# Seams of a two-layer diffusion block on one core: gate rows in pieces behind other products, projections and the last dense unit tile by tile, routing ahead of splits

## The chip, the cores and the metric

The kernel runs on one core of a Trainium2 chip. Its engines are TensorE (PE in the profile, with PEld for its weight loads), VectorE (DVE), ScalarE (ACT), GpSimd (POOL) and SyncE (SP, which here only issues transfers). The metric is the device time of one execution in microseconds (us).

## The reference

Two layers over 256 latent tokens x and 256 context tokens xc of width 1024, all in fp32:

```python
# even layer, for latent and context tokens (each with its own modulation)
h = modulate(rms_norm(x, norm_mix), sh1, sc1) @ w_in          # 1024 -> 2048
u, q, k, v = split(h)                                         # 4 x 128 Fourier groups | 8 heads of 64
q, k = rms_norm(q, q_gain), rms_norm(k, k_gain)
x = x + g1 * (concat(fourier_mix(u), attention(q, k, v)) @ w_out)
x = x + g2 * ((silu(h2 @ w1) * (h2 @ w3)) @ w2)               # h2 = modulate(rms_norm(x, ..)), width 2816
# odd layer, latent tokens only at its end
h = modulate(rms_norm(x, norm_mix), sh1, sc1) @ w_in          # attention (12/3 heads, rotary) | S5 recurrence
x = x + g1 * (concat(o_attn, o_ssm) @ w_out)
t = modulate(rms_norm(x, norm_ffn), sh2, sc2)
logits = t @ router_w + router_b; top 2 of 8, softmax over the two
x = x + g2 * sum_e gate_e * ((silu(t @ w1[e]) * (t @ w3[e])) @ w2[e])   # width 3584
```

`modulate(h, shift, scale)` is `h * (1 + scale) + shift`, and g1, g2 are gate vectors of width 1024 from the same conditioning.

## The kernel before

Tokens lie in four tiles of 128 (two latent, two context), features on the free side in X; SyncE streams all weights through a ring of three slots of 2 MB (six halves). Each engine's program is written out by hand, and semaphores join them; nothing is reordered by a scheduler. Dense and expert weights are split into two fp32r parts, WR (ScalarE, a copy) and rest (VectorE, a difference), and each product is three passes over them, in units of one ring half. Such a unit is written `split`, and three or four are prepared ahead of the dense part and of the experts.

The places that the change touches, in order of time:

- **q/k gains of the even layer.** GpSimd makes sixteen products of the S5 tables (L1870 to L1875, each stored by a transfer, L1876), then multiplies q and k by their gains (L1883, eight tiles, `head_ready`), then loads the biases of the attention (L1894). TensorE's transposes of q and k (L571) wait for the gains.
- **Gate rows.** A gate vector lies over partitions, in `mod`. To multiply with it, TensorE makes from it a row that is equal in all partitions (L656: four products of 128 columns into bank 7 for half a row) and ScalarE copies it out (L1134). `gate_rows(q)` makes all rows of gate q together: 4 for q = 0 and 1, 2 for q = 2 and 3. Each waits until ScalarE has emptied bank 7. They stand before the even and the odd output projection, before the dense part, and before the router's products.
- **Output projection** (`w_out`, L674). One bank of 128 tokens by 512 columns at a time, in banks 3 to 6 in turn: first the left half for all tiles, then the right half. VectorE multiplies each bank with its gate row (`gated_sum`, L1381) into one of two buffers, and GpSimd adds it to X (`residual`, L1760).
- **Norms.** `squares` (ScalarE) waits for all residuals, squares each tile and adds it up (L1034), then one Sqrt for all (L1024); `normed` (VectorE) makes mean, reciprocal (L1312, L1314) and scales the tiles (L1352); TensorE transposes them (`norm_turn`, L534, banks 0 to 3), ScalarE and VectorE modulate in turn (L1048, L1363), and ahead of the dense part they also split the result into hTr (L1054, L1369).
- **Dense part** (`dense_swiglu`). Units "up" (L695) and "down" (L713); the last unit goes over its two 128-row slices and, inside, over the four tiles, so that all four banks end together.
- **Routing.** VectorE clears acc, ye and part of pick (L1614 to L1616), makes two splits (L1594), then takes the logits (L892) and goes through top 2, ranks (L900) and the pick tables (L1714); TensorE gathers with them (L911), and the first expert begins (L938).

## Time and profile before

| | |
|---|---|
| Median of 3 runs | 2031.52 us (2027.45 to 2033.12) |
| The profiled execution's own time | 2027.75 us |
| Its span in the trace | 2026.0 us |
| Busy share PE / DVE / ACT / POOL | 93% / 61% / 48% / 15% |
| Mean granted TensorE clock | 0.964 of full speed |

Times in the trace are microseconds from the start of its span. The granted clock is 1.00 at 2.4 GHz and 0.50 at 1.2 GHz. A busy TensorE isn't TensorE at its peak: matmuls overlap, and their ends are modelled.

### The profile page before, as it was taken

The page shows a single profiled execution, that of the slowest core. Times are in us where ns is not written, and L with a number is a line of the kernel's source. Part 1 is how long each engine was busy: PE and PEld are TensorE (multiplying, and loading weights), DVE is VectorE, ACT ScalarE, POOL GpSimd, SP SyncE. Part 2 cuts the span into 40 slices and gives each one's busy share as a digit, 9 for nine tenths or more (in the row PEclk, how much of TensorE's full clock was granted, in tenths as well). Part 3 has the DMA queues.
Part 4 walks back from the last instruction along what each step waited for, and adds up shares of the span by engine and source line. Part 5 has one row for each costly group of instructions (what it writes and reads, how often), then busy time and mean ns, then how long its engine had stood idle before and what let it go on. Part 6 is the DMA issues. An engine that isn't in the chain of part 4 may idle for free.

```text
span 2026.0 us, 25076 instructions
## 1 busy us (share of the span) xinstructions
PE 1887.9 (93%) x8946; PEld 1422.5 (70%) x8946; DVE 1232.6 (61%) x1303; ACT 974.5 (48%) x1051; POOL 306.0 (15%) x584
## 2 busy tenths in 40 slices
PE   5999989699999996879599999999999999999997
PEld 3445554687878784645578888788887878878785
DVE  2121641333332322383688888988989889888996
ACT  2011330421222212243367777777776777776773
POOL 6887702002020202401000000000000000000000
PEclk8998999799999998989699999999999999999999
DMA  9254981122221225141189899998999989999994
GB/s 373 99 221 121 353 353 42 42 104 83 87 101 66 100 84 181 23 135 42 42 335 373 340 357 353 344 373 325 370 354 343 374 323 369 355 346 352 345 366 161
DMA packets 72087, 481.69 MB, mean 238 GB/s; under 512 B 8336, under 2 KB 11536, under 8 KB 17168
## 3 DMA queue, kind: packets, MB, share of 16 engines
q1 hardware_dynamic: 67888, 468.73, 60.7%
q0 software_dynamic: 2448, 7.61, 1.4%
q10 hardware_dynamic: 1680, 4.43, 0.6%
q8 instruction: 42, 0.69, 0.1%
q14 instruction: 29, 0.24, 0.0%
HBM read 473.41 MB, written 7.32 MB: 237 GB/s over the span
## 4 chain that ended last, share of the span: by engine, by line
PE 83%; POOL 7%; DVE 4%; issue 2%; ACT 2%; DMA 1%; ACTq 0%; DVEq 0%; POOLq 0%
PE bank L938 30%; PE bank L952 15%; PE bank L695 12%; PE bank L713 6%; PE bank L674 4%; PE bank L751 3%; PE bank L911 2%; PE bank L975 2%; PE bank L507 2%; PE bank L921 1%; PE bank L639 1%; PE bank L622 1%; POOL X L1760 1%; PE bank L656 1%; PE bank L534 1%
## 5 line engine op out<-in xcount | busy, mean ns | idle before, releaser
L1594 DVE TENSOR_TENSOR rest<-ring,WR 128x2048 fp32r<-128x2048 f32 x336 | 758.7, 2289 | 101.4 <-ACT WR L1214 100.9
L1214 ACT ACTIVATE WR<-ring 128x2048 fp32r<-128x2048 f32 x336 | 632.9, 1917 | 51.0 <-DMA ring<-in_experts 50.2
L938 PE MATMUL bank<-WR,xer 128*128 128x512 f32 x1792 | 588.0, 400 | 4.7 <-DVE xer L1682 4.7
L938 PEld LDWEIGHTS bank<-WR,xer 128*128 128x128 f32 x1792 | 337.7, 188 | 76.6 <-issue 8.8
L938 PE MATMUL bank<-rest,xer 128*128 128x512 f32 x896 | 350.5, 391 | 0.0
L952 PE MATMUL bank<-WR,heTr 128*128 128x512 f32 x896 | 281.9, 392 | 0.0
L695 PE MATMUL bank<-hTr,WR 128*128 128x512 f32 x704 | 222.0, 397 | 12.5 <-DVE tmpf L1381 12.5
L938 PEld LDWEIGHTS bank<-rest,xer 128*128 128x128 f32 x896 | 169.3, 189 | 36.2 <-issue 3.8
L952 PEld LDWEIGHTS bank<-WR,heTr 128*128 128x128 f32 x896 | 168.2, 188 | 34.3
L952 PE MATMUL bank<-rest,heTr 128*128 128x512 f32 x448 | 174.5, 389 | 0.0
L695 PEld LDWEIGHTS bank<-hTr,WR 128*128 128x128 f32 x704 | 135.2, 193 | 41.9 <-issue 13.7
L1471 DVE TENSOR_TENSOR rest<-ring,WR 128x2048 fp32r<-128x2048 f32 (+2 forms) x38 | 82.0, 2163 | 124.4 <-ACT WR L1149 124.4
L1977 POOL COPY gTe<-B 128x256 f32 x8 | 3.2, 402 | 989.5 <-PE bank L911 989.5
L695 PE MATMUL bank<-hTr,rest 128*128 128x512 f32 x352 | 139.2, 396 | 0.0
L1235 ACT ACTIVATE sile<-bank 128x256 f32<-128x256 f32 x112 | 43.0, 384 | 176.8 <-PE bank L938 176.8
L554 PE MATMUL bank<-ring,HT 128*128 128x512 f32 x256 | 111.6, 595 | 1.1 <-ACT HT L1048 1.1
L713 PE MATMUL bank<-WR,gTr 128*128 128x512 f32 x352 | 109.1, 389 | 0.0
L1760 POOL TENSOR_TENSOR X<-X,tmpf 128x512 f32<-128x512 f32 x32 | 52.2, 1665 | 358.8 <-DVE tmpf L1381 358.8
L952 PEld LDWEIGHTS bank<-rest,heTr 128*128 128x128 f32 x448 | 84.2, 188 | 16.7
L554 PEld LDWEIGHTS bank<-ring,HT 128*128 128x128 f32 x256 | 48.1, 190 | 61.7 <-issue 60.4
L1149 ACT ACTIVATE WR<-ring 128x2048 fp32r<-128x2048 f32 (+2 forms) x38 | 63.9, 1687 | 43.4 <-DMA ring<-in_ffn_up 43.4
L674 PE MATMUL bank<-ring,B 128*128 128x512 f32 x192 | 82.7, 592 | 0.0
(300 smaller groups left out, 1979.8 us busy)
## 6 DMA issues: line engine op xcount, KB each, us to landing
ring<-in_experts SPq DMA_DIRECT2D x336, 1024.0 KB, 4.8
ring<-in_ev_mod SPq DMA_DIRECT2D x24, 1024.0 KB, 9.2
ring<-in_od_mod SPq DMA_DIRECT2D x24, 1024.0 KB, 11.1
ring<-in_ffn_up SPq DMA_DIRECT2D x22, 1024.0 KB, 6.8
ring<-in_ffn_down SPq DMA_DIRECT2D x12, 768.0 KB, 5.3
ring<-in_ev_in SPq DMA_DIRECT2D x8, 1024.0 KB, 12.0
ring<-in_ev_out SPq DMA_DIRECT2D x4, 1024.0 KB, 10.6
ring<-in_od_out SPq DMA_DIRECT2D x4, 1024.0 KB, 13.1
```

The costliest lines, as they stand in the source:

```text
L554: mm = pe.matmul(bank[4 + j % 4][:, :], hT[:, c, t * P:(t + 1) * P], w[:, c, :], start=(c == 0), stop=(c == DC - 1))
L674: mm = pe.matmul(bank[3 + (half * tiles + t) % 4][:, :], oTv[:, c, t * P:(t + 1) * P], w[:, c, :], start=(c == 0), stop=(c == DC - 1))
L695: mm = pe.matmul(bank[2 * m + f][:, :], w[i][:, c, f * P:(f + 1) * P], hTr[:, j, c, :], start=(c == 0 and x == 0), stop=(c == DC - 1 and x ...
L713: mm = pe.matmul(bank[t + (4 if d == 0 else 0)][:, :], gTr[:, i, c, t * P:(t + 1) * P], w[j][:, k, :], start=(c == 0 and x == 0), stop=(c ...
L751: mm = pe.matmul(bank[4 + i % 4][:, 0:w_], hT[:, c, t * P:(t + 1) * P], w[:, c // 4, c % 4, :], start=(c == 0), stop=(c == DC - 1))
L938: mm = pe.matmul(bank[m % 2][:, :], xer[:, i, 4 * kh + k, :], w[j][:, 512 * k:512 * k + 512], start=(kh == 0 and k == 0 and x == 0), stop= ...
L952: mm = pe.matmul(bank[4 + h][:, :], heTr[:, i, c, :], w[j][:, D * k + 512 * h:D * k + 512 * h + 512], start=(c == 0 and x == 0), stop=(c = ...
L1149: act.activation(part(0, h, n), ring[:, h % HALVES, 0:n], ACT.Copy).then_inc(split_hi, 1)
L1214: act.activation(part(0, h), ring[:, h % HALVES, :], ACT.Copy).then_inc(split_hi, 1)
L1471: dve.tensor_tensor(part(1, h, n), ring[:, h % HALVES, 0:n], part(0, h, n).bitcast(F32), ALU.subtract).then_inc(split_lo, 1)
L1594: dve.tensor_tensor(part(1, h), ring[:, h % HALVES, :], part(0, h).bitcast(F32), ALU.subtract).then_inc(split_lo, 1)
L1760: pool.tensor_tensor(x, x, buf[:, r % 2, :], ALU.add).then_inc(res_done, 1)
```

## The change

Seven edits, none of which changes what is computed:

1. The q/k gains (now `gains(n)`) are put before products 11 and 14 of the S5 tables.
2. `gate_rows` becomes `gate_row(q, x)`, one half row. Those of the output projections follow its first four (two) banks, those of the dense part its first four units, and those of the experts the router's products.
3. Both output projections go tile by tile (both halves of a tile, then the next). Each residual and norm follows in that order: `squares` waits for the residuals of one tile, and root, mean and scaling are made per tile (`normed_tile`).
4. The last dense unit goes tile by tile, with a signal after each (`ffn_tail`), and VectorE gates and norms the tiles in turn.
5. The transposes ahead of the dense part use banks 4 to 7; its normed tiles lie in B.
6. A ScalarE instruction with Sqrt is issued ahead of the norm behind the dense part.
7. In routing, VectorE clears acc behind the selection, and ye, part of pick and the two splits come behind the pick tables.

```diff
@@ TensorE
-            def gate_rows(q):
+            def gate_row(q, x):
                 layer, m, streams = GATES[q]
-                k = 2 * sum(GATES[i][2] for i in range(q))
-                for s in range(streams):
-                    for half in range(2):
...
+                s, half = divmod(x, 2)
+                k = 2 * sum(GATES[i][2] for i in range(q)) + x
+                if k >= 1:
+                    pe.wait_ge(gate_ready, k)
...
-            def w_out(slot0, tiles, oTv, r0):
+            def w_out(slot0, tiles, oTv, r0, gate):
 
-                for half in range(2):
-                    wait_slot(pe, slot0 + half)
+                for b in range(2 * tiles):
+                    t, half = divmod(b, 2)
+                    if t == 0:
+                        wait_slot(pe, slot0 + half)
...
+                    if b >= 4:
+                        pe.wait_ge(res_gated, r0 + b - 3)
+                    for c in range(DC):
+                        mm = pe.matmul(bank[3 + b % 4][:, :], oTv[:, c, t * P:(t + 1) * P],
+                                       w[:, c, :], start=(c == 0), stop=(c == DC - 1))
+                    mm.then_inc(res_psum, 1)
+                    if b < tiles:
+                        gate_row(gate, b)
...
+                        if u == F_UNITS - 1:
+                            for t in range(TILES):
+                                for k in range(ks):
+                                    c = ks * kh + k
+                                    for x, (i, j) in enumerate(PASSES):
+                                        mm = pe.matmul(bank[t][:, :], gTr[:, i, c, t * P:(t + 1) * P], w[j][:, k, :],
+                                                       start=False, stop=(c == FG[q] - 1 and x == 2))
+                                if t < TILES - 1:
+                                    mm.then_inc(ffn_tail, 1)
...
                     mm.then_inc(unit_done, 1)
+                    if u < 4:
+                        gate_row(1, u)
...
-            gate_rows(0)
             pe.wait_ge(o_ready, len(EVEN_STEPS))
             pe.wait_ge(four_o, 8)
-            w_out(S_OUT_E, 4, oT, 0)
+            w_out(S_OUT_E, 4, oT, 0, 0)
             norm_turn(1)
-            gate_rows(1)
             dense_swiglu(8)
@@ ScalarE
...
                 for t in range(tiles):
-                    act.activation(XN(q)[:, t, :], X[:, t, :], ACT.Square,
+                    if q:
+                        act.wait_ge(res_done, before - (tiles - 1 - t if q == 2 else 2 * (tiles - 1 - t)))
...
+                    act.activation(XN(q, t), X[:, t, :], ACT.Square,
                                    accum_out=ss[:, t:t + 1]).then_inc(square_sum, 1)
-                root(rstd[:, 0:tiles])
+                    if q:
+                        root(rstd[:, t:t + 1])
@@ VectorE
+            def normed_tile(q, t):
+                dve.wait_ge(square_sum, sum(NORMS[i][3] for i in range(q)) + t + 1)
+                rsqrt_mean(rstd[:, t:t + 1], ss[:, t:t + 1], D)
+                dve.tensor_scalar(XN(q, t), X[:, t, :], rstd[:, t:t + 1], None, ALU.mult).then_inc(xn_ready, 1)
...
-            gated_sum(halves4[:2], 0, [3, 4], tmp, G, 4)
+            gated_sum(halves4[:2], 0, [3, 4], tmp, G, 0)
             split(0)
-            gated_sum(halves4[2:4], 2, [5, 6], tmp, G, 4)
+            gated_sum(halves4[2:4], 2, [5, 6], tmp, G, 0)
+            normed_tile(1, 0)
             split(1)
-            gated_sum(halves4[4:], 4, [3, 4, 5, 6], tmp, G, 4)
-            normed(1)
+            gated_sum(halves4[4:6], 4, [3, 4], tmp, G, 0)
+            normed_tile(1, 1)
+            gated_sum(halves4[6:], 6, [5, 6], tmp, G, 0)
+            normed_tile(1, 2)
+            normed_tile(1, 3)
...
-            normed(2)
+            for t in range(TILES):
+                dve.wait_ge(*((ffn_tail, t + 1) if t < TILES - 1 else (unit_done, F_UNITS)))
+                gated_sum([(1, t)], 4 + RES_FFN + t, [t], tmpf, GF, 8)
+                if t:
+                    normed_tile(2, t - 1)
+            normed_tile(2, TILES - 1)
@@ GpSimd
             for k in range(2 * PAIRS):
+                if k in (11, 14):
+                    gains((k - 11) // 3)
```

The first place is TensorE from the last attention product of the even layer (L639 before, L643 after) to the first dense product. Such lists count a product as written; the trace has two instructions for one in fp32. Before:

```order
L639 MATMUL bank<-S,B 64x128 x4
L656 MATMUL bank<-cst,mod 128x128 x16
L674 MATMUL bank<-ring,B 128x512 x64
L534 MATMUL bank<-cst,xnf 128x128 x32
L656 MATMUL bank<-cst,mod 128x128 x16
L695 MATMUL bank<-hTr,WR 128x512 x2
```

After:

```order
L643 MATMUL bank<-S,B 64x128 x4
L675 MATMUL bank<-ring,B 128x512 x8
L659 MATMUL bank<-cst,mod 128x128 x4
L675 MATMUL bank<-ring,B 128x512 x8
L659 MATMUL bank<-cst,mod 128x128 x4
L675 MATMUL bank<-ring,B 128x512 x8
L659 MATMUL bank<-cst,mod 128x128 x4
L675 MATMUL bank<-ring,B 128x512 x8
L659 MATMUL bank<-cst,mod 128x128 x4
L675 MATMUL bank<-ring,B 128x512 x32
L538 MATMUL bank<-cst,B 128x128 x32
L698 MATMUL bank<-hTr,WR 128x512 x2
```

The block of four gate rows (L656) in front of the projection is now four rows between its banks, and the block in front of the dense products is gone; its rows come one after each of the first four units.

The second place is VectorE at the end of the dense part, from its last split to the modulation of the odd layer. Before:

```order
L1471 TENSOR_TENSOR rest<-ring,WR 128x1024
L1381 TENSOR_TENSOR tmpf<-bank,GF 128x512 x8
L1312 TENSOR_SCALAR rstd<-ss 128x4
L1314 RECIPROCAL rstd<-rstd 128x4
L1352 TENSOR_SCALAR B<-X,rstd 128x1024 x4
```

After:

```order
L1494 TENSOR_TENSOR rest<-ring,WR 128x1024
L1404 TENSOR_TENSOR tmpf<-bank,GF 128x512 x6
L1330 TENSOR_SCALAR rstd<-ss 128x1
L1332 RECIPROCAL rstd<-rstd 128x1
L1376 TENSOR_SCALAR B<-X,rstd 128x1024
L1404 TENSOR_TENSOR tmpf<-bank,GF 128x512
L1330 TENSOR_SCALAR rstd<-ss 128x1
L1332 RECIPROCAL rstd<-rstd 128x1
L1376 TENSOR_SCALAR B<-X,rstd 128x1024
L1404 TENSOR_TENSOR tmpf<-bank,GF 128x512
```

Of the eight gatings (L1381, L1404) the last two now stand behind the norms of the tiles before them.

The third place is VectorE from the modulation of the last norm to the first expert's inputs. Before (between the "..." lies the selection, which is the same in both):

```order
L1363 TENSOR_SCALAR HT<-bank,coef,mod 128x256 x4
L1614 MEMSET X 128x2048
L1615 MEMSET B 128x1024
L1616 MEMSET B 128x2x128
L1594 TENSOR_TENSOR rest<-ring,WR 128x2048 x2
L1620 TENSOR_TENSOR s5v<-bank,vec 128x16
...
L1714 TENSOR_SCALAR B<-cst,s5v 128x128 x32
L1719 COPY B<-bank 128x512 x2
```

After:

```order
L1386 TENSOR_SCALAR HT<-bank,coef,mod 128x256 x4
L1649 TENSOR_TENSOR s5v<-bank,vec 128x16
...
L1666 MEMSET X 128x2048
...
L1744 TENSOR_SCALAR B<-cst,s5v 128x128 x32
L1748 MEMSET B 128x1024
L1749 MEMSET B 128x2x128
L1626 TENSOR_TENSOR rest<-ring,WR 128x2048 x2
L1754 COPY B<-bank 128x512 x2
```

The three memsets and two splits that stood in front of the first routing instruction (L1620, L1649) are now inside and behind it.

## Rows read from the trace of the kernel before

**Rows 1.** The page, part 4: shares of the chain that ended last, by engine.
```profile
PE 83%; POOL 7%; DVE 4%; issue 2%; ACT 2%; DMA 1%; ACTq 0%; DVEq 0%; POOLq 0%
```

**Rows 2.** Timeline, 163 to 201: start, us, engine, line, operation, [idle before <- releaser].
```profile
164.96 9.83 POOL L1883 TENSOR_TENSOR B<-B,vec 128x512 f32<-128x512 f32 x8
...
166.65 1.05 PE L520 MATMUL bank<-cst,S 128*128 128x2 f32 x8 [0.81 <-DVE S L1322]
...
169.94 3.93 PE L571 MATMUL bank<-cst,B 128*128 128x128 f32 x16 [2.24 <-POOL B L1883]
...
178.50 3.67 PE L585 MATMUL bank<-S,B 128*128 128x512 f32 x7
...
200.99 0.43 DVE L1438 TENSOR_TENSOR bank<-bank,S 128x256 f32<-128x256 f32 x1 [0.63 <-PE bank L608]
```

**Rows 3.** Timeline, gate rows and start of the even output projection.
```profile
292.15 0.97 PEld L656 LDWEIGHTS bank<-cst,mod 128*128 128x128 f32 x8 [0.17 <-issue]
...
298.74 55.10 PE L674 MATMUL bank<-ring,B 128*128 128x512 f32 x128
```

**Rows 4.** Timeline, last bank of the even output projection to the transposes.
```profile
353.87 0.69 DVE L1381 TENSOR_TENSOR S<-bank,S 128x512 f32<-128x512 f32 x1 [6.17 <-PE bank L674]
354.64 1.26 POOL L1760 TENSOR_TENSOR X<-X,S 128x512 f32<-128x512 f32 x1 [5.60 <-DVE S L1381]
...
359.07 1.04 ACT L1034 ACTIVATE xnf<-X 128x1024 f32<-128x1024 f32 x1
...
360.22 1.28 ACT L1024 ACT_TABLE_LOAD   x1
...
361.96 2.74 DVE L1352 TENSOR_SCALAR xnf<-X,rstd 128x1024 f32<-128x1024 f32 x4
...
364.76 6.57 PE L534 MATMUL bank<-cst,xnf 128*128 128x128 f32 x32 [10.93 <-DVE xnf L1352]
```

**Rows 5.** Timeline, the second residual of that projection, beside VectorE's first split.
```profile
313.44 3.24 POOL L1760 TENSOR_TENSOR X<-X,S 128x512 f32<-128x512 f32 x1 [5.53 <-DVE S L1381]
```

**Rows 6.** Timeline, last slices of the dense input and the first dense product.
```profile
374.63 1.42 DVE L1369 TENSOR_TENSOR hTr<-hf,hTr 128x512 fp32r<-128x512 f32 x2
...
382.19 1.20 PE L695 MATMUL bank<-hTr,WR 128*128 128x512 f32 x2
```

**Rows 7.** Timeline, first gating behind the last dense unit, and the transposes behind it.
```profile
761.21 1.29 DVE L1381 TENSOR_TENSOR tmpf<-bank,GF 128x512 f32<-128x512 f32 x2 [6.84 <-PE bank L713]
...
776.11 5.72 PE L534 MATMUL bank<-cst,B 128*128 128x128 f32 x32 [14.93 <-DVE B L1352]
```

**Rows 8.** Timeline, last gating of the odd output projection, and the transposes behind it.
```profile
962.39 0.69 DVE L1381 TENSOR_TENSOR S<-bank,S 128x512 f32<-128x512 f32 x1 [6.12 <-PE bank L674]
...
969.86 3.67 PE L534 MATMUL bank<-cst,B 128*128 128x128 f32 x16 [7.51 <-DVE B L1352]
```

**Rows 9.** Timeline, routing to the first expert product.
```profile
974.50 1.76 DVE L1614 MEMSET X<- 128x2048 f32 x1 [0.38 <-issue]
...
976.84 5.57 PE L892 MATMUL bank<-vec,HT 128*128 128x8 f32 x32
...
979.47 4.49 DVE L1594 TENSOR_TENSOR rest<-ring,WR 128x2048 fp32r<-128x2048 f32 x2 [1.86 <-ACT WR L1214]
...
989.27 0.17 DVE L1646 COPY s5v<-bank 128x16 f32<-128x16 f32 x1 [0.99 <-PE bank L900]
...
990.23 8.30 DVE L1714 TENSOR_SCALAR B<-cst,s5v 128x128 f32<-128x128 f32 x32 [0.19 <-issue]
...
1001.23 0.69 DVE L1719 COPY B<-bank 128x512 f32<-128x512 f32 x1 [2.70 <-PE bank L987]
...
1006.81 0.79 PE L938 MATMUL bank<-WR,xer 128*128 128x512 f32 x1 [4.74 <-DVE xer L1682]
```

**Rows 10.** Stretches: busy us and count by engine, granted clock, DMA share, GB/s.
```profile
976.00:978.00 2.00, 2.00 (x20) 2.00 (x20) 1.45 (x3) 0.96 (x2) 0.00 (x0) 1.00 0.00 0
978.00:980.00 2.00, 2.00 (x13) 2.00 (x12) 0.53 (x1) 2.00 (x2) 0.00 (x0) 0.56 0.00 0
```

More of the change, by code:

```diff
@@ new lines, in gate_row @@
+                k = 2 * sum(GATES[i][2] for i in range(q)) + x
+                if k >= 1:
+                    pe.wait_ge(gate_ready, k)
+                else:
+                    pe.wait_ge(four_o, 8)
+                for j in range(4):
+                    c = m + 4 * half + j
+                    mm = pe.matmul(bank[7][:, j * P:(j + 1) * P], mod[layer][:, c, s:s + 1].to_broadcast([P, P]), ident,
+                                   start=True, stop=True)
+                mm.then_inc(gate_psum, 1)
@@ L1463, in _ @@
             attention(EVEN_STEPS, 0, oT, 4)
-            halves4 = [(half, t) for half in range(2) for t in range(4)]
+            halves4 = [(half, t) for t in range(4) for half in range(2)]
             modulated(0, 32, 48, (1,))
@@ L1498, in _ @@
                                           ALU.subtract).then_inc(g_lo, 1)
-                if what[0] == "down" and what[3] == 1:
+                if what[0] == "down" and what[3] == 1 and u < F_UNITS - 1:
                     q, d = what[1:3]
@@ L1716, in experts @@
                     ins.then_inc(pick_ready, 1)
+                if rnd == 0:
+                    dve.memset(ye[:, :], 0.0).then_inc(y_dve, 1)
+                    dve.memset(pick[:, :, NE, :], 0.0)
+                    for u in range(2, AHEAD + 1):
+                        split_unit(0, u)
                 for g in range(1, 4, 2):
@@ L1961, in _ @@
                 ins.then_inc(head_ready, 1)
-            residual([(half, t) for half in range(2) for t in range(2)], 8 + RES_FFN, tmp)
+            residual([(half, t) for t in range(2) for half in range(2)], 8 + RES_FFN, tmp)
             def experts(rnd):
```

138 lines of the change are left out of this document (61 added, 77 removed).

## The prediction

> **What bounds the kernel now.** I read the shares of the chain that ended last first. Four fifths of it are TensorE, and the next entries are GpSimd and VectorE: small work that TensorE stands still for [rows 1]. So the question is only how long TensorE idles at the places that the diff touches, and I went through those in order of time with the timeline. There are four: the q/k gains before the even attention, the way from the even output projection to the dense part, the way from the dense part to the odd layer, and the way from the odd output projection through routing to the first expert. The products between them are not changed, so each earlier start at a place moves all behind it, down to the end, and the sum is a sum of shortened gaps.
>
> **Place 1, the q/k gains.** The eight gain multiplications on GpSimd stand behind all sixteen table products and start at 164.96; TensorE has ended its last small product at 166.65 + 1.05 = 167.70 and begins to transpose at 169.94 [rows 2]. The change puts them after the eleventh and fourteenth product, where their inputs are long there. GpSimd does the same work, but the order of who waits turns. Low bound: the start moves to 167.7 (2.2), and the 32 transposes with their waits, 169.94 to 178.50, shrink to twice 3.93, which is 0.7 more: 2.9. High bound: the clock stays at 2.4 GHz and they take half, 3.9: 2.2 + 8.6 - 3.9 = 6.9. They alternate between two banks that ScalarE and VectorE empty, which a faster clock doesn't speed, so I take 4.5. Cover lost: GpSimd's bias loads now stand directly behind the last table product and its store, where the gains (9.83) used to hide that store. Even 10 later, the first bias would be there well before its first use at 200.99 [rows 2] (now its loads start when the gains end, at 174.8), moved 4.5 forward.
>
> **Place 2, even projection to dense products.** Four terms.
> (a) The four gate rows stand as a block from 292.15 to 298.74, 6.6, and each is 0.97 of weight loads; the block is longer since every row waits for ScalarE to empty one bank [rows 3]. Now the projection starts when VectorE has copied the last attention tile, some 0.5 after 292.15, and a row follows each of the first four banks, four times 1.0. Gain 6.1 - 4.0 = 2.1. Two things queue behind it: ScalarE's first split now stands behind all four row copies (four banks of 55.10/8 = 6.9 and four rows of 1.0 after 292.65, so about 325 instead of 299), and VectorE's own split, hence the gating of the third bank, behind that (about 330). TensorE wants that bank's buffer with its seventh bank, at about 338: 8 to spare. The ring slot that the projection holds is freed after the seventh bank and not the fourth; the next weights are first split about 20 later, so I cost it at nothing.
> (b) The tail before the transposes is 353.87 to 364.76, 10.9: gate 0.8 to the residual, residual 1.3, four squares (about 1.1 each), a table load of 1.28 on ScalarE, root and reciprocal, four scalings, 2.74 together [rows 4]. With a root per tile only the last tile is left in it, and the table is loaded at the first tile: 0.8 + 1.3 + 1.15 + 0.65 (mean, root, reciprocal) + 0.8 (one scaling with its hand-off) = 4.7. To that I add 0.7: VectorE scales tile 2 just when GpSimd adds the last residual. A residual takes 1.26 alone and 3.24 beside VectorE's split [rows 4, 5]. That makes 5.4, gain 5.5. The Trainium skill (GPSIMD Engine Reference, the table of its specifications) says that GpSimd and VectorE share their SBUF interfaces, with contention when VectorE has two SBUF inputs or runs in a two-port mode. By that rule the 0.7 is charged; by the row alone, which shows only a split beside it, it could be nought and the gain 6.2. It is a rule against the tile-by-tile form, at three places, and small.
> (c) From the first transpose to the first dense product it is 364.76 to 382.19, 17.4, of which the transposes are 6.6 and the rest is gate rows and their waits [rows 4, 6]. With the rows gone and the transposes in banks 4 to 7 the products can start 6.6 after the first transpose. Their eighth slice is ready 376.05 - 364.76 = 11.3 after it [rows 6]; the first product reaches that slice after 6.6 + 7 x 0.7 = 11.5, so it doesn't wait. Gain 10.8.
> (d) Four rows come back behind the first four dense units: minus 4.0.
> Place 2: 2.1 + 5.5 + 10.8 - 4.0 = 14.4. Bounds: 12 (the products catch up with the slices, one more hand-off per row) and 16.
>
> **Place 3, dense to odd layer.** The gap is 761.21 to 776.11, 14.9 [rows 7]. The last unit now ends one bank after another, 6 products or 1.4 apart, so the first tile is done 4.1 earlier. VectorE does it in order, though, and each normed tile holds it for ScalarE's square and root. I follow it: bank 0 gated at 757.1, residual, square done 760.4, scaled 761.9; bank 2 gated, tile 1 scaled 764.2; bank 3 gated 764.9, residual 766.2, square 767.7, scaled 769.2. So the transposes start at about 769.3 instead of 776.1: 6.8. Low bound 5.4 (contention), high 9.5 (the tail of 5.4 as in 2b, nothing queued). I take 6.6.
>
> **Place 4, odd projection to experts.** Tail: 962.39 to 969.86 is 7.5 [rows 8]; by the terms of 2b without contention it becomes 4.7. Gain 2.8, and 0.5 for the two gate rows ahead of the projection, by the same reckoning as (a) with two rows. Routing: the logits now follow the modulation at once, 4.3 behind the first transpose (974.2 by the old times) instead of 976.84, and VectorE takes them up when they land instead of after its splits, at 983.96 [rows 9]. The 32 small products took 5.57, most of it at a granted 0.56 or less; in 976 to 978 at 1.00 TensorE got through 20 instructions in 2.0 [rows 10]. The clock had risen by then and fell since TensorE had idled for the rows; now it doesn't. So the logits land between 977.2 and 979.9: routing starts 4.1 to 6.8 earlier. What was in front comes back: a memset of 1.76, of which 1.0 vanishes in the wait for ranks (0.99), and behind the pick tables two memsets (1.2) and two splits (4.5), of which the wait of 2.70 for the transposes swallows 2.7 [rows 9]. Back: 0.8 + 3.0. Net 0.3 to 3.0, and by the clock row I take 2.4. Place 4: 5.7.
>
> **Sum.** 4.5 + 14.4 + 6.6 + 5.7 = 31.2. Bounds 2.9 + 12 + 5.4 + 3.1 = 23.4 and 6.9 + 16 + 9.5 + 6.5 = 38.9. The profiled execution took 2027.75 and becomes 1996.6. The three runs have a median of 2031.52, 3.8 above it; from it the sum gives 2000.3. I expect the new median between, at 1999.
>
> **The rivals.**
> *A, the waits only move.* VectorE, in order, now meets ScalarE seven more times in the tails, and if each meeting costs as much as the batch saved, 2b, place 3 and the tail of place 4 give nothing (5.5 + 6.6 + 2.8 = 14.9): a saving of 16.3, 2015. For it: in place 3 I already find VectorE late for banks 2 and 3. Against: a square, root and scaling of one tile are 2.6 in all, and in place 2 a bank comes only every 6.9.
> *B, the clock.* TensorE still idles about 5 to 8 at each place. After such a stop its clock was down to 0.56 in 978 to 980 [rows 10], so it can restart slow where I assumed neither gain nor loss. Two microseconds for each of four places: 8, saving 23, 2007.
> *C, slower.* The output projections serialise: if ScalarE's row copies or VectorE's gating stand in TensorE's way at every bank, each of 8 + 4 banks costs a round of product end, row copy and gating, about 2.5, that is 30, and with place 1 bringing nothing the kernel ends at 2031 or above. It decides once a bank waits more than 2.6. Against: four banks rotate, and I count 8 of slack at the tightest.
> *D, more.* Place 1 at its high bound and place 3 undelayed: 37, 1993.
>
> **How the numbers follow.** The forecast has 0.72, A 0.06, B 0.14, C 0.02, D 0.06. All but A and C lie within 1989 to 2009: the lower end is the high bound of the sum from the profiled time (1988.9), the upper the low bound from the median (2008.1). 0.3% is 6, about what three runs can tell from no change. Only C and part of A's neighbourhood fall short of that: faster 0.96, same 0.02, slower 0.02.
>
> **What would show it.** Transposes of q and k start within 0.5 of the last small product. The even projection starts about 6 earlier and ends 2 to 3 earlier against the attention's end. From the last gating to the first transpose: 5.4, 8.1 and 4.7 at places 2, 3 and 4 (from 10.9, 14.9, 7.5), with no table load in them. First dense product 6.6 behind the first transpose. Router products under 3.5 in all, and first expert product 34.5 behind the first transpose of place 4 instead of 37.0 [rows 8, 9]. Wrong would be: a bank of the projection that waits for gating, a first expert product that is not earlier against the transposes, or a gap at the first use of a bias.

## The result, and the profile after

The changed kernel takes 1999.88 us (median of 4 runs, 1995.87 to 2001.87), the kernel before beside it 2032.32 (4 runs, 2027.45 to 2034.21): ratio 0.9842, 95% interval 0.9818 to 0.9865. The forecast was 1999.0, between 1989 and 2009.

| | before | after |
|---|---|---|
| The profiled execution's own time | 2027.75 us | 1995.87 us |
| Its span in the trace | 2026.0 us | 1994.0 us |
| Busy share PE / DVE / ACT / POOL | 93% / 61% / 48% / 15% | 94% / 62% / 49% / 15% |
| Mean granted TensorE clock | 0.964 | 0.973 |

The page's shares of the chain, the answer to [rows 1]: GpSimd has gone from 7% to 1%, VectorE has 5% instead of 4%.

```profile
PE 90%; DVE 5%; ACT 2%; issue 2%; DMA 1%; POOL 1%; ACTq 0%; DVEq 0%
```

Both traces read at the same events give the saving by place. A gap is counted from the last work ahead of it to the first behind it.

| term | forecast | measured in the two traces |
|---|---|---|
| place 1, q/k gains | 4.5 | 5.8 at the Fourier products, 4.7 left at the attention's end |
| 2a, gate rows in the even projection | 2.1 | 2.4 |
| 2b, last gating to first transpose | 5.5 | 6.2 (10.9 to 4.7) |
| 2c, first transpose to first dense product | 10.8 | 11.7 (17.4 to 5.8) |
| 2d, dense part with its rows | -4.0 | -4.1 |
| place 3, end of the last unit to first transpose | 6.6 | 7.2 (14.9 to 7.7) |
| place 4, rows / tail / routing | 0.5 / 2.8 / 2.4 | 0.5 / 2.8 / 0.6 |
| sum, before rounding | 31.2 | 31.9 (with 4.7 for place 1); the spans differ by 32.0 |

Both profiled executions are the fastest of their kernel, 4.6 below the median before and 4.0 below it after.

Place 1, timeline of TensorE in the changed kernel (start, us, engine, line, operation, [idle before <- releaser], as in [rows 2]):

```profile
166.53 1.05 PE L524 MATMUL bank<-cst,S 128*128 128x2 f32 x8 [0.81 <-DVE S L1340]
167.44 1.07 PE L575 MATMUL bank<-cst,B 128*128 128x128 f32 x8
...
170.20 2.70 PE L575 MATMUL bank<-cst,B 128*128 128x128 f32 x16 [0.18 <-ACT HT L1089]
172.74 2.74 PE L589 MATMUL bank<-S,B 128*128 128x512 f32 x6
```

The transposes follow the last small product with no wait on GpSimd, and 32 of them take 5.3 instead of 8.6: only the two copies behind them hold them now, and the clock is at 1.00 from 166 to 172, where before had 0.50 from 170 to 178, behind its wait.

Place 2, the answer to [rows 3, 4, 6]: end of the attention, last bank, norm, and first dense products. PE L538 are the transposes, L698 the dense products.

```profile
286.90 0.66 PE L643 MATMUL bank<-S,B 128*64 128x128 f32 x8
287.97 2.41 PE L675 MATMUL bank<-ring,B 128*128 128x512 f32 x5 [0.42 <-DVE B L1480]
...
346.84 0.69 DVE L1404 TENSOR_TENSOR S<-bank,S 128x512 f32<-128x512 f32 x1 [6.17 <-PE bank L675]
347.61 1.26 POOL L1795 TENSOR_TENSOR X<-X,S 128x512 f32<-128x512 f32 x1 [5.60 <-DVE S L1404]
348.06 1.36 DVE L1376 TENSOR_SCALAR B<-X,rstd 128x1024 f32<-128x1024 f32 x1
348.90 1.06 ACT L1050 ACTIVATE B<-X 128x1024 f32<-128x1024 f32 x1 [1.08 <-POOL X L1795]
...
351.52 6.01 PE L538 MATMUL bank<-cst,B 128*128 128x128 f32 x32 [4.77 <-DVE B L1376]
357.29 0.70 PE L698 MATMUL bank<-hTr,WR 128*128 128x512 f32 x2
...
362.14 0.73 PE L698 MATMUL bank<-hTr,WR 128*128 128x512 f32 x2 [0.48 <-DVE hTr L1392]
```

The projection starts 1.07 behind the start of the last value products, where it was 7.18. From the last gating to the transposes everything is one tile's chain, with no table load in it. Two details matter. Tile 2 is scaled beside GpSimd's residual and takes 1.36, where the next tile's scaling at 350.71 takes 0.75, but the residual takes its 1.26 all the same, and the square behind it waits for nothing else. And the dense products catch up with the slices once, for 0.48.

Place 4, VectorE, ScalarE and TensorE in routing, the answer to [rows 9]:

```profile
938.34 3.68 PE L538 MATMUL bank<-cst,B 128*128 128x128 f32 x16 [4.77 <-DVE B L1376]
942.74 3.87 PE L904 MATMUL bank<-vec,HT 128*128 128x8 f32 x32 [0.73 <-DVE HT L1386]
946.64 0.17 DVE L1649 TENSOR_TENSOR s5v<-bank,vec 128x16 f32<-128x16 f32 x1 [4.05 <-PE bank L904]
950.15 1.76 DVE L1666 MEMSET X<- 128x2048 f32 x1 [0.43 <-issue]
951.37 0.60 ACT L1151 ACTIVATE B<-bank 128x512 f32<-128x512 f32 x1 [2.16 <-PE bank L659]
951.99 1.28 ACT L1245 ACT_TABLE_LOAD   x1
953.28 0.20 ACT L1245 ACTIVATE s5v<-s5v 128x2 f32<-128x2 f32 x1
953.51 0.17 DVE L1669 TENSOR_SCALAR s5v<-s5v 128x2 f32<-128x2 f32 x1 [1.60 <-ACT s5v L1245]
955.58 8.29 DVE L1744 TENSOR_SCALAR B<-cst,s5v 128x128 f32<-128x128 f32 x32 [0.19 <-issue]
965.13 4.42 DVE L1626 TENSOR_TENSOR rest<-ring,WR 128x2048 fp32r<-128x2048 f32 x2
969.48 1.27 DVE L1754 COPY B<-bank 128x512 f32<-128x512 f32 x2
974.67 0.79 PE L952 MATMUL bank<-WR,xer 128*128 128x512 f32 x1 [7.66 <-DVE xer L1712]
```

Counted from the first transpose, the selection starts at 8.3 instead of 14.0, but the pick tables at 17.2 instead of 20.4 and the first expert product at 36.3 instead of 37.0. So the lead is 5.7 at the selection, 3.1 at the pick tables and 0.6 at the expert. It is lost in three rows: the memset (1.76), a wait of 1.60 for the Exp, which stands on ScalarE behind two row copies and its table load, and the splits, of which only a part hides a wait.

### The profile page after: what moved, and what is told of

Same layout as the page of the kernel before. It is cut to its first block, busy times and chain, and to the rows that moved or that the text cites. A ratio compares the mean times of both kernels' runs of the same rounds, so it can differ in the third digit from the quotient of the medians.

```text
span 1994.0 us, 25123 instructions
## 1 busy us (share of the span) xinstructions
PE 1878.3 (94%) x8946; PEld 1414.1 (71%) x8946; DVE 1236.5 (62%) x1317; ACT 976.2 (49%) x1059; POOL 298.7 (15%) x584
## 4 chain that ended last, share of the span: by engine, by line
PE 90%; DVE 5%; ACT 2%; issue 2%; DMA 1%; POOL 1%; ACTq 0%; DVEq 0%
PE bank L952 31%; PE bank L966 15%; PE bank L698 12%; PE bank L727 6%; PE bank L558 6%; PE bank L675 4%; PE bank L765 3%; PE bank L511 2%; PE bank L989 2%; PE bank L925 1%; DMA X<-in_ctx 1%; PE bank L935 1%; PE bank L643 1%; PE bank L626 1%; PE bank L589 1%
## 5 line engine op out<-in xcount | busy, mean ns | idle before, releaser
L952 PEld LDWEIGHTS bank<-WR,xer 128*128 128x128 f32 x1792 | 337.8, 188 | 79.5 <-issue 11.7
L698 PE MATMUL bank<-hTr,WR 128*128 128x512 f32 x704 | 221.9, 397 | 13.2 <-DVE tmpf L1404 12.7
L698 PEld LDWEIGHTS bank<-hTr,WR 128*128 128x128 f32 x704 | 134.3, 192 | 42.7 <-issue 13.9
L698 PE MATMUL bank<-hTr,rest 128*128 128x512 f32 x352 | 139.1, 395 | 0.0
L727 PE MATMUL bank<-WR,gTr 128*128 128x512 f32 x336 | 104.1, 389 | 0.0
## 6 DMA issues: line engine op xcount, KB each, us to landing
ring<-in_od_mod SPq DMA_DIRECT2D x24, 1024.0 KB, 10.1
```

The source lines that it names most:

```text
L698: mm = pe.matmul(bank[2 * m + f][:, :], w[i][:, c, f * P:(f + 1) * P], hTr[:, j, c, :], start=(c == 0 and x == 0), stop=(c == DC - 1 and x ...
L727: mm = pe.matmul(bank[t + (4 if d == 0 else 0)][:, :], gTr[:, i, c, t * P:(t + 1) * P], w[j][:, k, :], start=(c == 0 and x == 0), stop=(c ...
L952: mm = pe.matmul(bank[m % 2][:, :], xer[:, i, 4 * kh + k, :], w[j][:, 512 * k:512 * k + 512], start=(kh == 0 and k == 0 and x == 0), stop= ...
```

## The experiments

Each kernel ran five rounds beside the kernel before. A ratio to before is known to about 0.2%, 4 us, so terms of 1 to 6 us are read as gaps in the traces, one of each kernel, and the medians only have to agree. "After" is the changed kernel; sizes are us.

**Gains behind all table products again** (gains_back).

```diff
             for k in range(2 * PAIRS):
-                if k in (11, 14):
-                    gains((k - 11) // 3)
...
+            gains(0)
+            gains(1)
             load_bias(0)
```

> The q/k gains stand behind all table products again; all other edits stay. Theory: place 1 is worth 4.7 net. The changed kernel gained 6.3 up to the first scores and gave 1.6 back inside the even attention, where the clock fell to 0.50 in 244 to 246 after TensorE had waited 1.10 for a conditioning row. With the gains back the transposes wait 2.2 again, the fall is gone, and the time is 1999.9 + 4.7 = 2004.6. Rival: the fall has nothing to do with where the gains stand; it shows here too (or is chance), and the edit's worth is its full 6.3: 2006.2 or more.

2007.54 (4 runs, 2004.65 to 2009.69), ratio 0.9883 (0.9863 to 0.9904): 7.7 above after. TensorE's rows:

```profile
168.10 1.05 PE L524 MATMUL bank<-cst,S 128*128 128x2 f32 x8 [0.81 <-DVE S L1340]
171.47 3.94 PE L575 MATMUL bank<-cst,B 128*128 128x128 f32 x16 [2.31 <-POOL B L1896]
176.37 3.87 PE L575 MATMUL bank<-cst,B 128*128 128x128 f32 x16 [0.96 <-POOL B L1896]
```

From the last small product to the first scores it is 33.1, in after 27.0, in before 33.2: the edit is worth 6.1 there. What after gave back in the attention was a fall of the clock in its own profile (busy us and count by engine, granted clock, DMA share, GB/s):

```profile
244.00:246.00 2.00, 2.00 (x15) 0.27 (x7) 1.25 (x2) 0.00 (x0) 1.92 (x3) 0.50 0.85 352
```

It isn't bound to the edit. The eleven kernels below all have the gains moved, and their attention takes between 90.3 and 93.6 from the first scores to the last value products (after 93.3); this one has 92.0 and before 91.7. My theory of 4.7 fell; the gap of 6.1 is near the rival's 6.3, and the median lies above both.

**The dense part's gate rows as a block again** (rows_block).

```diff
             norm_turn(1)
+            for x in range(4):
+                gate_row(1, x)
             dense_swiglu(8)
...
                     mm.then_inc(unit_done, 1)
-                    if u < 4:
-                        gate_row(1, u)
```

> The four gate rows of the dense part stand as a block between transposes and first dense product again (in bank 3, so that they need not wait for the transposes' banks); all other edits stay. Theory: each row waits for ScalarE, which first ends its modulation (362.0 in the changed kernel), then copies 0.6 a row with a row of 1.0 between: the first dense product comes at about 368.5 and not 357.3, 11.2 later; back come 4.1 (no rows in the dense part) and 0.5 (no wait for slices). Net +6.6: 2006.5. Rival: the rows cost only their own 4.1 wherever they stand, since the first product would wait for slices anyway: +0 to +0.5, 2000.

2010.02 (5 runs, 2006.81 to 2012.05), ratio 0.9895 (0.9877 to 0.9912): 10.1 above after.

```profile
355.15 6.67 PE L538 MATMUL bank<-cst,B 128*128 128x128 f32 x32 [4.77 <-DVE B L1378]
361.65 1.06 PE L659 MATMUL bank<-cst,mod 128*128 128x128 f32 x8
366.25 1.16 PE L659 MATMUL bank<-cst,mod 128*128 128x128 f32 x8 [3.54 <-ACT GF L1153]
368.09 2.08 PE L659 MATMUL bank<-cst,mod 128*128 128x128 f32 x8 [0.69 <-ACT GF L1153]
370.85 2.07 PE L659 MATMUL bank<-cst,mod 128*128 128x128 f32 x8 [0.69 <-ACT GF L1153]
372.58 1.20 PE L700 MATMUL bank<-hTr,WR 128*128 128x512 f32 x2
```

First transpose to first dense product is 17.4, as in before, against 5.8: with the rows in front, nothing of term 2c is left. They cost 4 as work, and the rest is waiting for ScalarE, which copies the first only behind its modulation; the stops also bring TensorE to half clock, where a row takes 2.08 instead of 1.06. "Only their own 4.1" is refuted. The theory's 6.6 in all was too small as well: of the 4.1 that should have come back in the dense part only 2.9 did (380.2 from its first product to its last, after 383.1), for here it begins at half clock.

**Transposes ahead of the dense part in banks 0 to 3 again** (banks03).

```diff
-                        mm = pe.transpose(bank[k % 4 + (4 if q == 1 else 0)][:, t * P:(t + 1) * P], ...
+                        mm = pe.transpose(bank[k % 4][:, t * P:(t + 1) * P], ...
...
             norm_turn(1)
+            wait_ht(1)
             dense_swiglu(8)
```

> The transposes ahead of the dense part use banks 0 to 3 again, and the first dense product, which writes bank 0, waits until all of them are modulated; all other edits stay. Theory: the last modulation ends at 361.4, so the first product starts 4.1 later, saves its wait for slices (0.5), and the time is 3.6 longer: 2003.5. Rival: the slices set the pace either way and the products catch up with them: +0.5 at most, 2000.4.

2006.36 (4 runs, 2003.60 to 2008.78), ratio 0.9878 (0.9858 to 0.9898).

```profile
351.55 6.55 PE L538 MATMUL bank<-cst,B 128*128 128x128 f32 x32 [4.77 <-DVE B L1377]
361.54 1.19 PE L698 MATMUL bank<-hTr,WR 128*128 128x512 f32 x2 [3.45 <-ACT hf L1068]
```

The first product comes 10.0 behind the first transpose instead of 5.8, 4.2 later, near the theory's 4.1. So moving the rows pays in full only with the banks moved too. The median is 6.5 above after and not 3.6: behind the longer stop the dense part begins at half clock (361.5 to 367.6) and takes 385.9 instead of 383.1.

**Norms of all tiles at once** (batch_norms): squares wait for the last residual, one root, one `normed(q)`.

```diff
-                    if q:
-                        act.wait_ge(res_done, before - (tiles - 1 - t if q == 2 else 2 * (tiles - 1 - t)))
+                    if q and t == 0:
+                        act.wait_ge(res_done, before)
...
-                    if q:
-                        root(rstd[:, t:t + 1])
...
-            normed_tile(1, 2)
-            normed_tile(1, 3)
+            normed(1)
```

> Squares, root and scaling of the three norms are made for all tiles at once again, behind the last residual; the banks still come tile by tile. Theory: the per-tile form is worth, from the last gating to the first transpose, 6.2 at place 2 (four squares 4.2, a table load of 1.28 and four scalings of 2.7 come back), 2.9 at place 3 (the table is preloaded there, and VectorE is free for its gatings), 2.8 at place 4: +11.9, 2011.8. Rival A of the prediction, the meetings cost what the batch saved: no change, 2000. If most of it is in place 2, the trace shows it there.

2013.64 (5 runs, 2011.96 to 2015.41), ratio 0.9911 (0.9894 to 0.9927). The gaps from the last gating to the transposes are 10.9 at place 2 (after: 4.7) and 7.5 at place 4 (4.7); at place 3 TensorE idles 9.85 instead of 7.69. Together 11.2 for the 11.9 expected; the median rose by 13.8. Rival A is refuted: the meetings of VectorE and ScalarE cost far less than the batch. In this trace routing, which the edit doesn't touch, has the clock at 0.50 from 952 to 983 and takes 39.5 from the first transpose to the first expert product; in after it is 36.3.

**VectorE's old order in routing** (routing_old): memsets and both splits ahead of the logits.

```diff
+            dve.memset(acc[:, :, :], 0.0)
+            dve.memset(ye[:, :], 0.0).then_inc(y_dve, 1)
+            dve.memset(pick[:, :, NE, :], 0.0)
+            for u in range(2, AHEAD + 1):
+                split_unit(0, u)
             top = s5v[:, R_T, :]
             dve.wait_ge(logits, 1)
```

> VectorE's order in routing is that of before (three memsets and two splits ahead of the logits); the router's products stay ahead of the gate rows, and all other edits stay. Theory, from the rows of the changed kernel (first transpose 938.34): memsets to 945.5, splits to 950.1, so the selection starts 3.5 later than 946.64, but it needs no wait for Exp (1.6) and no memset (1.76) inside, the pick tables start 0.8 later, and the tables' transposes are waited for instead of hiding splits: copies at about 967.8 instead of 969.5. First expert product 34.7 behind the first transpose and not 36.3; 1998.3. So of the routing edits only the move of the logits ahead of the rows would be worth anything. Rival (the prediction's step): routing ahead of the splits is itself worth 2.4 less what the Exp wait took, so undoing it costs 0.6 to 2.4: 2000.5 to 2002.3, first expert product 36.9 or more behind the transpose.

1996.64 (5 runs, 1994.10 to 1999.67), ratio 0.9829 (0.9811 to 0.9848), 3.2 below after, which the intervals alone don't separate. In the trace the first expert product is 35.5 behind the first transpose, with after at 36.3 and before at 37.0:

```profile
938.75 3.67 PE L538 MATMUL bank<-cst,B 128*128 128x128 f32 x16 [4.77 <-DVE B L1376]
...
957.11 8.29 DVE L1748 TENSOR_SCALAR B<-cst,s5v 128x128 f32<-128x128 f32 x32 [0.19 <-issue]
968.75 0.69 DVE L1753 COPY B<-bank 128x512 f32<-128x512 f32 x1 [3.35 <-PE bank L1001]
974.24 0.79 PE L952 MATMUL bank<-WR,xer 128*128 128x512 f32 x1 [4.65 <-DVE xer L1716]
```

The pick tables start 1.1 later than in after, and the copies behind them wait 3.35 for TensorE, time in which after's splits only partly fit. So the logits ahead of the gate rows are worth 1.5, and the new order of VectorE costs 0.8 of it. The 0.8 is more than chance moves this gap in most traces: six with after's routing have 36.3 to 36.5. Two others, batch_norms and slice_major, have 39.5 at half clock.

**Routing mended** (routing_mended).

```diff
@@ ScalarE
-            for x in range(2):
-                gate_row(3, x)
+            act.activation(warm[:, 0:1], cst[:, C_ONE:C_ONE + 1], ACT.Exp)
             act.wait_ge(top_gap, 1)
             act.activation(s5v[:, R_T, 4:6], s5v[:, R_T, 2:4], ACT.Exp).then_inc(top_exp, 1)
+            for x in range(2):
+                gate_row(3, x)
@@ VectorE: the three memsets ahead of dve.wait_ge(logits, 1), and
                 gathered((NE + 1) * rnd)
-                for u in range(AHEAD + 1) if rnd else ():
+                for u in range(AHEAD + 1) if rnd else range(2, AHEAD + 1):
```

On TensorE the two rows stand behind the ranks.

> Routing mended by its rows: the three memsets stand in VectorE's idle 4.05 before the logits, an Exp of one column loads ScalarE's table before it is wanted, the two gate rows (TensorE and ScalarE) come behind the ranks and the Exp, and the two splits behind the first expert's inputs. Theory: the Exp wait of 1.60 and the memset of 1.76 leave the path, of which a wait for ranks takes back 0.5 (2.9 gained), and the splits and memsets behind the tables (5.6) leave it down to the wait for the tables' transposes (2.4 gained): first expert product 31.0 behind the first transpose instead of 36.3, time 1994.6. Rival: the late splits (4.4) are wanted by the first expert's third unit, and its products wait there: the gain of 2.4 comes back as a gap within 20 us of the expert's start, 1997.

1994.23 (5 runs, 1992.29 to 1995.93), ratio 0.9813 (0.9796 to 0.9830), 5.7 below after, with intervals that still overlap. First transpose to first expert product: 31.7, for 31.0 expected, and 4.7 less than in after.

```profile
942.43 3.29 PE L538 MATMUL bank<-cst,B 128*128 128x128 f32 x16 [4.77 <-DVE B L1377]
...
953.82 0.17 DVE L1672 TENSOR_SCALAR s5v<-s5v 128x2 f32<-128x2 f32 x1 [0.27 <-ACT s5v L1244]
956.85 8.30 DVE L1747 TENSOR_SCALAR B<-cst,s5v 128x128 f32<-128x128 f32 x32 [0.19 <-issue]
974.10 0.79 PE L952 MATMUL bank<-WR,xer 128*128 128x512 f32 x1 [4.65 <-DVE xer L1715]
```

Now ScalarE waits for VectorE and not the other way round. The late splits are done by 980.5, while the first expert still works on its first units (its first Silu is at 981.2), and no gap follows: the rival of a gap is refuted.

**The last dense unit over its slices** (slice_major), each tile signalled behind its last product.

```diff
-                            for t in range(TILES):
-                                for k in range(ks):
+                            for k in range(ks):
+                                for t in range(TILES):
```

> The last dense unit goes over its two slices and, inside, over the tiles, each tile signalled behind its last product (0.7 apart instead of 1.4); norms per tile and all else stay. Theory: the first tile is done 2.1 later, VectorE's chain of gatings and norms is in order, so all of it shifts; I follow it to a first transpose 2.3 later (unit end to transpose 10.0 instead of 7.7): 2002.2. Rival: the last bank sets the end whatever the tiles before it do, since its end is not moved: no change, 1999.9.

**Two gatings ahead of the first norm** (dense_tail): g0 g1 g2 n0 g3 n1 n2 n3.

```diff
-                if t:
-                    normed_tile(2, t - 1)
-            normed_tile(2, TILES - 1)
+                if t >= 2:
+                    normed_tile(2, t - 2)
+            normed_tile(2, TILES - 2)
+            normed_tile(2, TILES - 1)
```

> Behind the last dense unit VectorE gates bank 2 before it norms tile 0, and bank 3 before tile 1 (g0 g1 g2 n0 g3 n1 n2 n3). Theory: at place 3 the last gating is late for VectorE's order (743.44, with the bank done at 740.4), not for TensorE or GpSimd. It then comes at 741.3, the last scaling ends 1.8 earlier: unit end to first transpose 5.9 instead of 7.7, 1998.1. Rival: GpSimd's residuals or ScalarE's squares and roots (each root waits for VectorE's mean) are the bound, and the order changes nothing: 1999.9.

**Without the extra Sqrt** (no_sqrt).

```diff
-            act.activation(warm[:, 0:1], cst[:, C_ONE:C_ONE + 1], ACT.Sqrt)
             squares(2)
```

> The changed kernel without the extra Sqrt ahead of the norm behind the dense part. Theory: the table load of 1.28 moves to the root of tile 0, and VectorE, in order, meets ScalarE there: all its later gatings and norms shift, unit end to first transpose 9.0 instead of 7.7, 2001.2. Rival: the load hides in ScalarE's idle time (15.4 before the first square) or in VectorE's waits, as it did at the other two norms, which have no extra Sqrt: 1999.9.

The three give 2005.34 (2001.98 to 2006.80; ratio 0.9866, 0.9848 to 0.9884), 2001.70 (2000.22 to 2002.57; 0.9849, 0.9833 to 0.9866) and 2000.68 (6 runs, 1999.66 to 2009.13; 0.9853, 0.9829 to 0.9877). The idle time of TensorE ahead of the odd layer's transposes, in after, slice_major, dense_tail and no_sqrt, one fence each:

```profile
748.10 5.40 PE L538 MATMUL bank<-cst,B 128*128 128x128 f32 x32 [7.69 <-DVE B L1376]
```

```profile
753.56 6.57 PE L538 MATMUL bank<-cst,B 128*128 128x128 f32 x32 [9.74 <-DVE B L1376]
```

```profile
751.78 6.39 PE L538 MATMUL bank<-cst,B 128*128 128x128 f32 x32 [6.57 <-DVE B L1376]
```

```profile
747.50 6.53 PE L538 MATMUL bank<-cst,B 128*128 128x128 f32 x32 [8.79 <-DVE B L1375]
```

The 7.69 is the same in all seven traces with after's order there and nothing in the wait. Every tile before the last counts, since VectorE goes through them in order: slices inside tiles cost 2.05 (2.3 expected), the table load 1.1 (1.3), and the better order gains 1.1 (1.8). The rest of the last went to contention: the scaling that stands ahead of the last gating runs beside GpSimd's residual and takes 1.38 instead of 0.75. slice_major's median is 5.5 above after; beside the gap's 2.05 its trace has 3.1 more in routing, at half clock from 944 to 974. All three rivals ("no change") are refuted by these gaps; dense_tail's gain doesn't show in its median, which lies 1.8 above after. Its trace has the clock at 0.50 from 286 to 296, 5.1 lost, where after has nothing.

**Unread products in TensorE's waits** (dummies), on top of routing_mended.

```diff
+            def dummy(b, n):
+                for _ in range(n):
+                    pe.matmul(bank[b][:, :], ident, cst[:, 0:512], start=True, stop=True)
...
             w_out(S_OUT_E, 4, oT, 0, 0)
+            dummy(0, 5)
             norm_turn(1)
```

and in the same way 8, 5, 3 and 5 at the other four waits.

> On top of routing_mended, products of 128 columns by 512 whose result nobody reads stand in TensorE's waits (some 0.86 each at full clock): 5 behind the even projection (wait 4.8), 8 behind the dense part (7.7), 5 behind the odd projection (4.8), 3 behind the router's products (3.0), 5 ahead of the first expert (4.65). Theory (rival B of the prediction, the clock): the stops themselves lower the clock, and what follows them is slower by it. With the waits filled it stays at 1.00: 0.5 less at place 2 (the slices bound it), 1.0 at place 3, and at place 4 0.7 to the logits, 1.0 on the ranks, 1.5 on the gather, 1.4 at the expert's start: about 6, 1988. Rival: the clock falls there all the same, or the transposes are bound by the modulation behind them (a slice every 0.85) and the gather by the pick tables: 1994, and no gap shorter than in routing_mended.

1990.63 (5 runs, 1986.74 to 1991.80), ratio 0.9793 (0.9770 to 0.9817), 3.6 below routing_mended. They help at three waits and not at two. Transposes to dense product take 5.1 (routing_mended 6.3), transposes to the odd layer's products 5.0 (7.1), and the first expert starts at full clock, where routing_mended has 0.50 for its first 2.9 (974.1 to 977.0), which is 1.4 lost. In routing nothing is gained (32.1 against 31.7): the clock falls in the router's small products, behind a wait of 0.73 only, 5.54 for 32 of them instead of 4.00, and again in the gather.

```profile
747.93 3.83 PE L543 MATMUL bank<-cst,B 128*128 128x128 f32 x32 [0.83 <-DVE B L1388]
939.11 5.54 PE L913 MATMUL bank<-vec,HT 128*128 128x8 f32 x32 [0.73 <-DVE HT L1398]
968.23 0.49 PE L962 MATMUL bank<-WR,xer 128*128 128x512 f32 x1 [0.36 <-DVE xer L1726]
```

**One such product ahead of each of the attention's last two value products** (attn_cover), on top of routing_mended.

```diff
+                    if steps is EVEN_STEPS and r >= n:
+                        dummy(2 * n % 3, 1)
                     if r >= 2:
                         pe_pv(steps[r - 2], j0 + r - 2)
```

> On top of routing_mended, one such product stands ahead of each of the even attention's last two value products, in TensorE's last waits there (1.2 and 0.9). Theory: with the gate rows moved, the projection follows the attention's thin end directly, and in eight of nine profiles of kernels with that order the clock is at 0.50 somewhere in the last 5 us before the projection or its first 8, for 1.7 to 5.1 of lost time (3.4 in routing_mended), where it was at 1.00 in before. With the waits filled it stays at 1.00 from 280 to 300: 1991.5. Rival: these short waits do not decide it (two profiles have the same waits and no fall there); the fall comes in this one too, and the time is 1994 to 1995.

1993.73 (5 runs, 1993.24 to 1995.91), ratio 0.9813 (0.9790 to 0.9837). Two stretches of routing_mended, then of attn_cover (busy us and count by engine, granted clock, DMA share, GB/s):

```profile
286.00:288.00 2.00, 2.00 (x15) 1.95 (x14) 0.00 (x0) 0.23 (x1) 0.00 (x0) 0.50 0.98 410
288.00:290.00 2.00, 1.58 (x6) 0.70 (x3) 1.39 (x8) 0.00 (x0) 0.00 (x0) 0.50 1.01 422
```

```profile
286.00:288.00 2.00, 2.00 (x18) 1.58 (x14) 0.29 (x1) 0.66 (x2) 0.00 (x0) 1.00 1.05 438
288.00:290.00 2.00, 1.58 (x11) 0.71 (x10) 0.73 (x4) 0.00 (x0) 0.00 (x0) 1.00 0.98 410
```

The fall is gone, and the median is lower by 0.5 only. One reason is in the trace: the second product fills no wait.

```profile
287.43 1.10 PE L530 MATMUL bank<-cst 128*128 128x512 f32 x2
288.47 0.66 PE L650 MATMUL bank<-S,B 128*64 128x128 f32 x8
```

The last value products start 2.93 behind those before them, where no_sqrt has 1.96 (283.10 and 285.06), both at full clock: it costs 1.0. The expectation's wait of 0.9 ahead of them isn't there at full clock. And no_sqrt and after, without these products, have no fall either. Open: see below.

**Together** (combined): routing_mended, dense_tail, attn_cover, and unread products at three waits (5, 6, 5).

> What the runs found, put together: routing_mended, the order of dense_tail behind the last dense unit, the products of attn_cover, and unread products in the waits ahead of the even layer's second transposes (5), of the odd layer's first (6) and of the first expert (5), but none between the odd projection and the gather, where they brought nothing. Theory: the parts add up. From routing_mended's 1994.2: 1.1 by dense_tail's gap, 1.1 at place 2, 1.9 at place 3 and 1.4 at the expert's start by the clock: 1988.7, and from the transposes ahead of routing to the first expert 31.7 as in routing_mended. Rival: a fall of the clock that is kept from one place comes at the next, so that dummies' saving of 3.6 is all there is: 1990 to 1991.

1988.27 (5 runs, 1985.95 to 1988.72), ratio 0.9779 (0.9758 to 0.9799): faster than both kernels of the case, by 11.6 than after. The sum of the theory was 1988.7. Its parts show at places 2 and 3 (5.1 from the transposes to the dense product, idle 6.6 behind the dense part, 5.0 from transposes to products), but routing took 33.9 instead of 31.7, at half clock from 936 to 960. So the rival is right in part: at that place the clock took 2.2 back.

## Why the prediction was right, point by point

*Place 1* was mis-sized: 4.5 for 5.8 to 6.1. That the sum needs only 4.7 for it is luck: a fall of the clock later in the attention took the rest back. The wait went as forecast (2.2). The 32 transposes went from 8.6 to 5.3, and the failed step is "a faster clock doesn't speed" them: the two copies (0.60 and 0.69) alternate and hold TensorE for only 0.2 at a time, so the end at full clock was the nearer one. Five of the later traces have a fall here and take 6.3. "A gap at the first use of a bias" did not come: VectorE's first use is at 194.73, 1.2 behind the first scores, as before.

*2a* was right by 0.3 where the clock stays up. From the last value products to the last gating it is 62.3 in before, and exactly 59.9 in the four traces without a fall; it is 61.3 to 63.1 in the nine changed kernels with one. There the term is worth 1.0 at most, and in the worst case less than nothing. No bank of the projection waited for gating in after, so rival C had no ground; I had put ScalarE's first split at 325 and it came at 319.8.

*2b* was right but for the 0.7 for contention: 4.68, not 5.4. The Trainium skill (GPSIMD Engine Reference, the table of its specifications) has VectorE and GpSimd share their SBUF interfaces, with contention when VectorE's instruction has two SBUF inputs or runs in a two-port mode. The trace agrees that they contend, 1.36 for 0.75; in which mode the scaling ran, no run shows. The step that failed was who pays: the slow instruction was VectorE's scaling of tile 2, off the path, and not GpSimd's residual. The order of their starts tells the two cases apart. In [rows 5] VectorE's split had started first, at 313.28, and GpSimd's residual, from 313.44, took 3.24; here the residual had started first, at 347.61, and the scaling, from 348.06, was the slow one. The scalings of place 3 (742.15 behind a residual at 741.70, 744.80 behind one at 744.19) fit too, with 1.36 and 1.20: in these rows whoever starts second pays. The first of those two stands right ahead of the last gating and does cost, as does dense_tail's 1.38; behind the second VectorE waits for ScalarE anyway.

*2c* was right (10.8 for 11.7). "It doesn't wait" for slices was wrong by 0.48: the eighth slice is ready 11.3 behind the first transpose, as forecast, but the products begin at 5.8 and not 6.6, and so are early for the seventh, which is ready at 10.6. rows_block and banks03 show the two conditions of this term, one edit each: 11.7 and 4.2.

*Place 3* was right in mechanism and size: 7.2 for 6.6, with VectorE late for banks 2 and 3 as I had followed it. slice_major, dense_tail and no_sqrt move it in the directions that this chain says.

*Place 4*, tail and rows, was right to 0.1. Routing was the step that failed: 0.6 for 2.4, and both its signs ("router products under 3.5 in all", "first expert product 34.5 behind the first transpose") came out wrong, with 3.87 and 36.3. The first half held: the selection starts 5.7 earlier, within the 4.1 to 6.8. (The clock was at 1.00 for nearly all of the 3.87, so the row of 20 instructions in 2.0 was too low a price.) Of this lead 3.8 was to go back, and 5.1 did: 2.6 up to the pick tables instead of 0.8, and 2.5 behind them instead of 3.0. I had the 0.8 for the memset, but not that the Exp stands behind two row copies, which stand behind two rows at half clock, and behind its table load. routing_old shows that the order of VectorE which the change brings is itself a loss of 0.8; routing_mended, which takes only these rows out of the way, gains 4.7 there.

The sum came out right (31.2 for 32.0) in part by luck, with errors against each other: places 2 and 3 too small by 2.4, routing too large by 1.8. Rival B had its mechanism right: by dummies the restart at half clock costs 1.2, 2.1 and 1.4 at three places. But the kernel before had it too (in 364 to 372, 776 to 782 and 1006 to 1012 its granted clock begins at 0.50), so it is no loss against it. Rival D held in neither part: place 1 came between the forecast and its high bound, and place 3 was delayed as I had followed it.

## What to carry to other kernels

Work that an engine does for another (here: rows that TensorE makes and ScalarE copies) costs its wait and not its duration when it stands as a block at a seam; behind products that run anyway it costs its duration, if the banks it shares are free as well. When a step is moved earlier on one engine, follow the answer that it asks of another: what stands ahead of that answer there, with its table load, decides. And where engines take turns over tiles, the order of the one that is busiest sets the end, so every tile's tail counts and not the last one's alone.

## What the runs showed of the hardware

The granted clock falls to 0.50 at short stops (in after at 243.0, behind a wait of 1.10), and at which of them differs from trace to trace of the same instructions. Fourteen traces of nearly the same attention range from 90.3 to 93.6, in part by it: the shortest three have no stretch at half clock between these events, the longest four have 6.5 and more of it. attn_cover and combined have none of it either and take 92.0 and 92.4, 1.0 of it for their second product. From 280 to 300, around the start of the even projection, 9 of the 11 changed kernels without attn_cover's products show such a fall, worth 1.7 to 5.1, and before does not, with its four gate rows there. attn_cover and combined, with their two added products, show none, nor do after and no_sqrt without them. That is consistent with the rows having been a cover whose loss takes back a part of term 2a, but two traces with those products don't settle it, and the medians (1993.73 and 1994.23) can't.

A busy TensorE is not safe from the fall: in dummies the router's products of 8 columns began at 1.00, behind a wait of 0.73, and with TensorE busy for all of 940 to 946 the clock was at 0.67 in the first 2 us and then at 0.50. Products of 512 columns ahead of a stretch kept it up at three other places.
